# Decoder step on one core: the input projection's first phase in chunks of 256, 384 and 392 tokens, and a three-operand step in the top-k search

## The reference

```
h = rms_norm(x) @ w_in                      # (1032, 1024) x (1024, 4168)
# columns: q 512, k 256, v 256, gate 512, index q 512, index w 8, index k 64, hgrn q/f/i/gate 4x512
score[t, s] = sum over 8 heads of relu(iq[t] . ik[s]) * iw[t]      # s <= t
keep the top 256 of score[t]                 # everything is kept for t < 256
attention over the kept keys, with a relative-position bias
HGRN2 recurrence over q, log-decay, k, v     # 8 heads, 64 x 64 state, chunkwise
y = x + (both branches, gated) @ w_out
```

## Time and profile before

| what | us |
|---|---|
| median of 3 runs | 795.87 |
| the three runs | 795.87, 800.88, 794.12 |
| profiled execution, its own time | 794.41 |
| its span, first to last instruction | 792.4 |
| TensorE busy in the span | 755.5 |
| VectorE / ScalarE / GpSimd busy | 550.4 / 420.8 / 389.2 |

### The profile page before, as it was taken

How to read it: one execution, slowest core, us unless ns; L and a number is a source line. 1 busy time by engine, 2 the same in 40 slices (tenths; PEclk the granted TensorE clock), 3 DMA queues, 4 the chain that set the end, 5 groups by cost and what they waited for, 6 DMA issues and landing times.

```text
span 792.4 us, 20225 instructions
## 1 busy us (share of the span) xinstructions
PE 755.5 (95%) x7576; PEld 699.6 (88%) x7576; DVE 550.4 (69%) x1114; ACT 420.8 (53%) x1274; POOL 389.2 (49%) x572
## 2 busy tenths in 40 slices
PE   3999999999999989999999999989899998999998
PEld 3889989899999989999989999967788877998998
DVE  3644767999989999878997847786746368554121
ACT  6765675336465857768465746654435564421110
POOL 3454735437825296548667255239861427510320
PEclk9999999999999999999999999999999999999999
DMA  8303021211102202041203445395583634441632
GB/s 286 93 21 88 14 88 38 74 55 55 55 2 82 93 23 100 29 128 48 95 2 89 140 115 168 90 284 147 149 242 124 202 124 136 136 131 61 230 95 87
DMA packets 69927, 83.57 MB, mean 105 GB/s; under 512 B 20458, under 2 KB 55962, under 8 KB 69578
## 3 DMA queue, kind: packets, MB, share of 16 engines
q1 hardware_dynamic: 65146, 68.68, 27.7%
q0 software_dynamic: 4688, 13.64, 6.1%
HBM read 64.95 MB, written 17.34 MB: 104 GB/s over the span
## 4 chain that ended last, share of the span: by engine, by line
PE 67%; DVE 11%; issue 8%; ACT 5%; POOL 5%; DMA 3%; SPq 0%; DVEq 0%; ACTq 0%; POOLq 0%
PE psum L2330 16%; PE psum L2327 13%; PE psum L1360 11%; PE psum L2246 4%; PE psum L1293 4%; PE psum L1309 3%; DVE flag_count L2066 2%; POOL w_low L555 2%; DMA page_keys<-in_cache_kt 2%; PE psum L1266 1%; PE psum L1272 1%; PE psum L1270 1%; DVE bit_kept L2079 1%; PE psum L2204 1%; PE psum L2182 1%
## 5 line engine op out<-in xcount | busy, mean ns | idle before, releaser
L2330 PE MATMUL psum<-w_high,xT_high 128*128 128x256 f32 x640 | 183.2, 286 | 3.6 <-ACT psum L1838 3.2
L2330 PE MATMUL psum<-w_low,xT_high 128*128 128x256 f32 x640 | 179.5, 280 | 0.0
L2330 PE MATMUL psum<-w_high,xT_low 128*128 128x256 f32 x640 | 179.3, 280 | 0.0
L555 POOL TENSOR_TENSOR w_low<-w_raw,w_high 128x256 fp32r<-128x256 f32 (+1 forms) x144 | 106.5, 778 | 64.6 <-ACT w_high L1715 55.0
L2330 PEld LDWEIGHTS psum<-w_high,xT_high 128*128 128x128 f32 x640 | 120.3, 188 | 6.2 <-ACT psum L1838 3.8
L2330 PEld LDWEIGHTS psum<-w_high,xT_low 128*128 128x128 f32 x640 | 120.4, 188 | 0.4
L2330 PEld LDWEIGHTS psum<-w_low,xT_high 128*128 128x128 f32 x640 | 120.5, 188 | 0.0
L2327 PE MATMUL psum<-xT_high,w_high 128*128 128x384 f32 (+3 forms) x312 | 102.8, 330 | 1.1 <-POOL w_low L555 1.1
L2327 PE MATMUL psum<-xT_low,w_high 128*128 128x384 f32 (+3 forms) x312 | 99.7, 319 | 0.0
L2327 PE MATMUL psum<-xT_high,w_low 128*128 128x384 f32 (+3 forms) x312 | 99.6, 319 | 0.0
L2066 DVE TENSOR_SCALAR_CACHE_REDUCE flag_count<-scores,candidate 128x512 f16<-128x512 f32 (+2 forms) x96 | 96.8, 1009 | 0.0
(11 more groups left out here) (335 smaller groups left out, 1847.7 us busy)
## 6 DMA issues: line engine op xcount, KB each, us to landing
w_raw<-in_w_main SPq DMA_DIRECT2D x40, 512.0 KB, 5.2
x_rows<-in_x_prompt SPq DMA_DIRECT2D x8, 512.0 KB, 6.0
page_keys<-in_cache_kt SPq DMA_DIRECT2D x32, 128.0 KB, 3.5
page_keys<-in_cache_kt POOLq DMA_DIRECT2D x32, 128.0 KB, 3.4
page_values<-in_cache_v SPq DMA_DIRECT2D x32, 128.0 KB, 3.8
page_values<-in_cache_v POOLq DMA_DIRECT2D x32, 128.0 KB, 3.8
x_res<-in_x_prompt SPq DMA_DIRECT2D x32, 128.0 KB
out<-y_rows SPq DMA_DIRECT2D x32, 128.0 KB
```

The costliest lines, as they stand in the source:

```text
L555: last = gp.tensor_tensor(WL[:, u % 2, 4 * h + k, 0:w], raw(u)[:, h, k, 0:w], f(WH[:, u % 2, 4 * h + k, 0:w]), ALU.subtract)
L2330: last = pe.matmul(ps(BANK[n], w, rows(i)), x[:, k, row0(i):row0(i) + rows(i)], ww[:, sl, k, 0:w], start=first, stop=final)
```

## The change

- Token chunks are 256, 384 and 392 wide instead of 384, 384 and 264.
- The index-query units have no job for the first chunk: seven jobs in the front instead of nine, four T jobs instead of six in the second iq unit. Job numbers after that are lower by four.
- Squares of row tiles 3 and 8 (the samples) are made by VectorE with a multiply-and-reduce of two operands, the other seven stay on ScalarE. ScalarE scales tiles 4 and 7, VectorE the others.
- The transposes of chunk 1 stand in one piece behind job 0, those of chunk 2 in two pieces, inside and behind job 3.
- SyncE starts the page table's two transfers before the weights of unit 1.
- GpSimd's order becomes: split 0, gathers (0; 0, 1), split 1, (0; 2 to 4), constants, split 2, (0; 5 to 7), (1; 0, 1), split 3, (1; 2 to 7), (2; all), (3; all), split 4, diagonal masks. The first job of unit 1 waits for half of split 1 only.
- `sample_index` is behind job 19, the last before unit 4, and its sum behind job 20, the first of unit 4. Three of the samples' flags are summed one job later than the shift by four would put them.
- The kept bit of the search: `tensor_scalar` with a constant and a per-partition scalar becomes `scalar_tensor_tensor` with the bit value broadcast as a second tensor.

```diff
-CHUNKS = [(0, 384), (384, 384), (768, 264)]
+CHUNKS = [(0, 256), (256, 384), (640, 392)]
+CHUNK_ROWS = [(0, 1), (2, 3, 4), (5, 6, 7, 8)]
+SQUARES_BY_ACT = [0, 1, 2, 4, 5, 6, 7]
+ROWS_BY_ACT = [4, 7]
...
-FRONT = [(x, b, c) for c in range(3) for x, b in ((0, 0), (1, 0), (1, 1))]
-IX_JOBS = 7
+FRONT = [(x, b, c) for c in range(3) for x, b in ((0, 0), (1, 0), (1, 1)) if x == 0 or c > 0]
+IX_JOBS = 5
...
-X_AT = {(2, 3): (1, range(4)), (2, 7): (1, range(4, 8)), (4, 7): (2, range(4)), (5, 3): (2, range(4, 8))}
+X_AT = {(0, 7): (1, range(8)), (3, 3): (2, range(4)), (3, 7): (2, range(4, 8))}
...
-        out = [(u, "T", b, c) for c in range(3) for b in range(2)]
+        out = [(u, "T", b, c) for c in (1, 2) for b in range(2)]
...
-GROUPS = {8: [0], 9: [1], 10: [2], 11: [3], 12: [4], 13: [5, 6], 15: [7], 16: [8], 17: [9], 18: [10], 19: [11]}
+GROUPS = {6: [0], 7: [1], 8: [2], 9: [3, 4], 11: [5, 6], 12: [7], 13: [8, 9], 14: [10], 15: [11]}
-KEYS_ROWS_AT, SAMPLE_AT, SAMPLE_SUM_AT = 7, 22, 23
-FLAGS_AT = {29: 0, 36: 1, 42: 2, 46: 3, 49: 4, 53: 5, 72: 6, 77: 7}
+KEYS_ROWS_AT, SAMPLE_AT, SAMPLE_SUM_AT = 5, 19, 20
+FLAGS_AT = {26: 0, 32: 1, 38: 2, 42: 3, 46: 4, 50: 5, 69: 6, 73: 7}
...
             load_x(0)
             sp.dma_start(IDN[:, :], c_ident).then_inc(s["ident_in"], 16)
             load_weights(sp, 0)
...
-            load_weights(sp, 1)
             load_x(1)
-            load_x(2)
...
+            load_weights(sp, 1)
+            load_x(2)
...
             split_w(gp, 0)
-            split_w(gp, 1)
             gp.wait_ge(s["page_rows_in"], 32)
...
-            load_index_keys(0, 0, NPG)
+            load_index_keys(0, 0, 2)
+            gp.wait_ge(s["x_rows_scaled"], 4)
+            split_w(gp, 1)
+            load_index_keys(0, 2, 5)
             gp.wait_ge(s["const_in"], CONSTS_IN)
...
-            load_index_keys(1, 0, 3)
+            split_w(gp, 2)
             gp.wait_ge(s["x_low_ready"], 3 * KC)
             gp.tensor_tensor(XS[:, :, :], f(XH[:, :, T:TT]), f(XL[:, :, T:TT]), ALU.add).then_inc(s["x_sample_ready"], 1)
-            split_w(gp, 2)
-            load_index_keys(1, 3, NPG)
-            load_index_keys(2, 0, 3)
+            load_index_keys(0, 5, NPG)
+            load_index_keys(1, 0, 2)
             split_w(gp, 3)
-            load_index_keys(2, 3, NPG)
+            load_index_keys(1, 2, NPG)
+            load_index_keys(2, 0, NPG)
             load_index_keys(3, 0, NPG)
...
                 if u == 3:
+                    split_w(gp, u + 1)
                     for t in range(2, NT):
...
-                    split_w(gp, u + 1)
...
+            def square(i):
+                r = rows(i)
+                dve.wait_ge(s[f"x_in{i}"], 16)
+                link(dve.tensor_tensor_reduce(CU[0:r, 0:D].bitcast(BF16), x_buf(i)[0:r], x_buf(i)[0:r], 1.0, 0.0, ALU.mult, ALU.add,
+                                              accum_out=STAT[0:r, 0, i:i + 1]))
...
-                    dve.tensor_scalar(HIT[:, 0:6], CNT[:, 0:6], float(TOPK), BITF[:, bass.ds(it, 1)],
-                                      ALU.is_lt, ALU.mult).then_inc(s["dve_chain"], 1)
+                    dve.scalar_tensor_tensor(HIT[:, 0:6], CNT[:, 0:6], float(TOPK), BITF[:, bass.ds(it, 1)].to_broadcast([P, 6]),
+                                             ALU.is_lt, ALU.mult).then_inc(s["dve_chain"], 1)
```

64 lines of the change are left out of this document (32 added, 32 removed).

## The result

The changed kernel took **803.65 us** (median of 15 runs, 795.5 to 808.96), the kernel before 799.13 us (15 runs, 794.12 to 800.88): a ratio of 1.0074, 95% interval [1.0053, 1.0094]. It is slower, by less than 1%, and outside the range of 783 to 801 that was forecast (794.0).

The account below looks back on a forecast made before the run. TensorE, busy 95%, was taken as the bound, with VectorE already setting its time at one place. 794.4 - 11.2 (matmuls) + 0.5 (front) + 5.8 (gathers and split) + 4.5 (VectorE's chain) gave 794.0 us, range 783 to 801.

Parts of the forecast that it names:

- the term of +4.5 us for VectorE's chain: VectorE's search and scans: TensorE waits 4.5 us for them up to pair 1.
- 6.5 us of the kept bit's waits: First 16 search rounds: of 7.9 us of waits above the floor, the new form saves 6.5.
- the front: TensorE up to the second iq unit: that unit starts at 56.2 us, 5.1 of 5.6 us kept, term +0.5.
- GpSimd's row: GpSimd's gathers and splits: split 2 starts at 46.7 us, gathers end at 136.6, then split 4 takes 5.6.
- T: Start of unit 4's first job, which needs split 4: forecast 142.4 us, bounds 136.5 and 152.
- matmuls: TensorE: 4 blocks x 24 matmuls x 256 tokens dropped, 11.2 us less.
- waiting for gathers and split: TensorE idle at `sample_index` and at unit 4's first job: +5.8 us.
- VectorE, the search: VectorE's search starts behind split 4 and the masks, at T + 2.1 = 144.5 us, 7.4 later than before.
- the late T: Rival: GpSimd's stream slower than before; T of 152 gives 803 us; decides from T = 142.8; chance 0.14.
- the bit that waits: Rival: the three-operand kept bit waits as long; 6.5 us come back at the second scan, 800 us; chance 0.12.
- Waits at the pairs: GpSimd's exponents for pair 0 come 11 us late; TensorE loses 4 to 5, its remaining gain at pair 1.
- The work removed stays removed: Rival: gathers end by 130 us, pairs 0 and 1 don't hold TensorE; 783.7 us, or 780.7; chance 0.22.

Follow-up runs that it names:

- after_again: The changed kernel, unedited, run and profiled again: median 807.15 us, ratio 1.0124 to before; its profiled execution took 809.7 us.
- bit_alone: The kernel before with only the kept bit in the new three-operand form: 796.41 us, ratio 0.9970 to before.
- first execution: The first profiled execution of the changed kernel: 795.5 us, the fastest of its 15.
- gaps: The changed kernel with a semaphore link after each GpSimd instruction of decayed keys, index queries' scale and splits: 805.95 us, ratio 1.0098 to before.
- gaps_first: woven_gathers with links between GpSimd's instructions only in the first pair's scale and the split behind it: 784.97 us, ratio 0.9838 to before.
- warm: The changed kernel with matmuls nobody reads, 24 before sample_index's wait and 10 before unit 4's first job: 807.08 us, ratio 1.0104 to before.
- old_bit: The changed kernel with the kept bit back in the old tensor_scalar form: 803.11 us, ratio 1.0058 to before.
- free_gathers: The changed kernel without each gather's wait for the one before it on its buffer: 789.24 us, ratio 0.9898 to before.
- woven_gathers: The changed kernel with the last sixteen gathers taken in turn from the third and fourth buffer, waits kept: 791.22 us, ratio 0.9918 to before.
- gaps_before: The kernel before with links after each GpSimd instruction of decayed keys, index queries' scale and splits: 796.69 us, ratio 0.9994 to before.
- free_before: The kernel before without each gather's wait for the one before it on its buffer: 807.89 us, ratio 1.0141 to before.
- gaps_free: free_gathers with the semaphore links of gaps between GpSimd's instructions: 806.19 us, ratio 1.0109 to before.

## Why the prediction was wrong

The sign of the mechanism was named: GpSimd's gathers late, TensorE idle at `sample_index` and at unit 4's first job. The step that failed is the term of +4.5 us for VectorE's chain. It could be that small only because 6.5 us of the kept bit's waits had been taken off the chain as saved by the new form, and they are not saved: the longest wait is 7.99 us in `after_again` and 7.37 in `bit_alone`, 7.36 before. Two more terms were too small: the front (+0.5 for 3 to 4) and, through it, GpSimd's row, so that T came 5.2 to 6.7 us late. Here is the sum, execution against execution, from the 794.4 us of the profiled one of before; the last term is what the others leave:

| term, us | forecast | first execution | `after_again` |
|---|---|---|---|
| matmuls | -11.2 | -11.2 | -11.2 |
| front | +0.5 | +4.1 | +3.0 |
| waiting for gathers and split | +5.8 | +5.9 | +8.5 |
| VectorE's chain up to pair 1, and all behind | +4.5 | +2.3 | +15.0 |
| sum | -0.4 | +1.1 | +15.3 |

The last term has both causes in it: in `after_again` the second scan stands at 287.94, not at 274.5, of which +6.7 are unit 4 (149.06 for T = 142.4), -0.6 the masks behind it and +7.4 the stretch from search to second scan. In the first execution a bit slipped through, and the term was small. Neither execution is a usual one. Against the median, 803.65, the forecast missed by 9.65 us: 4.7 are the base, since the profiled execution of before lay that far below its median of 799.13 (I had put the difference at 1.5 from three runs), and 4.9 are the mechanism. How these divide between the bit and the late T no run separates: with the bit's waits gone the time fell by 2 us at most in `gaps`, and by some 6 in `gaps_first`, where T was no longer late.

**TensorE's work**: 96 matmuls gone, right. **The start**: 11.10 us, forecast 11.0. **The front**: wrong by 3.6. I had the second iq unit start at 56.2, and it did at 59.83 (58.75 in `after_again`); of the 5.1 us to be kept, 1.5 were (2.6). Chunk 1's transposes began at 22.50, not at 20.5, because ScalarE waited for unit 1's weights, which now come behind the other loads:

```profile
19.02 1.06 ACT L1720 ACTIVATE w_high<-w_raw 128x1024 fp32r<-128x1024 f32 x1 [2.73 <-DMA w_raw<-in_w_main]
```

I had costed the page table's transfers at 1.4 us of SyncE's time and called them covered. SyncE issued unit 1's weights at 8.46 (before at 4.88), behind the page table and behind chunk 1's three tiles of 512 KB, which the prediction does not mention; and just ahead of the wait's end the DMA queues moved 12 GB/s. The kernel before has such a hollow as well, but behind its weights. Windows of the changed kernel and of before, as under `warm`, the last two numbers being the DMA engines' share and GB/s:

```profile
11.50:14.00 2.50, 2.50 (x14) 2.50 (x13) 2.46 (x6) 2.14 (x6) 2.50 (x6) 1.00 0.07 12
```

```profile
17.50:20.00 2.50, 2.50 (x16) 2.03 (x15) 1.86 (x4) 2.50 (x6) 2.50 (x4) 1.00 0.20 40
```

That is argued from the traces; no run had the loads in another order. Another 2 us went in chunk 2 (ix done at 49.7, not 45.6): its two rows of transposes took 2.38 us each where the sum has 1.94, and TensorE waited 0.44 us for the second half of split 1.

**GpSimd**, mis-sized for the same reason. Split 2 began at 50.82, not 46.7: +4.1. The rest of the row was well sized in this execution: five gathers 12.6 us (12.5), split 3 8.16 (7.5), 22 gathers 64.3 us from 77.72 to 142.01 (63.8), split 4 5.5 (the forecast's last addition, 136.6 + 5.6, is 142.2 and not 142.4, which changes nothing). So T = 147.57 in the first execution, and 5.2 us is 4.1 of the front with small change. In `after_again` split 2 began at 49.74 (+3.0), and the row itself took longer: five gathers +0.9, split 3 8.05, 22 gathers 66.06 us (3.00 each, +2.3), so T = 149.06. That a late ScalarE moves GpSimd's whole row, I had not followed further than my own estimate of 46.7.

**VectorE, the search**: T + 1.5 in both executions (2.1). **The kept bit** is the step that failed in kind. "Of these I take 6.5" was a saving that does not exist: 15.0 us for 31 bits in the first execution and 23.3 in the second, before 24.5; 7.99 in one of the second's. Its argument was that line 2082 never took over 0.61 us; but line 2082 runs right behind the bit, when GpSimd's run is over. The row of 7.36 us told the cause, GpSimd's run; what it did not tell is that the form had to do with it, and the rival on this, at 0.12, came true. The Trainium skill, SBUF — State Buffer, "Who interferes with whom", has a VectorE instruction with two SBUF inputs contend with GpSimd's reads: by that rule the new form would still wait, and the runs agree. Where it says that the pair is held for one whole instruction, the wait of 7.99 us, through all that was left of a run of twelve, is longer.

Two rivals came together: the late T (its point was T = 142.8) and the bit that waits. Each was given its own chance, 0.14 and 0.12, and each its own time, 803 and 800, as if one excluded the other; both together give about 807 at the T that was measured. Only with T = 152 would they give 809, so the 809.7 of `after_again` is met by this only roughly. The execution of 795.5 us, which has no long wait at the first pair, is near what the forecast described; it is the fastest of 15, and its like in `old_bit` (795.71) says that this is luck with one bit and not the form.

**Waits at the pairs**: right in place. GpSimd's exponents held ScalarE for 8.10 us at pair 0 (forecast some 10) and 5.71 at pair 1; TensorE lost 2.86 and 0.65 us behind it, less than the 4 to 5 taken. In `after_again` the second of them was 11.06 us and TensorE's wait 4.46.

**"The work removed stays removed"** (783.7): 8.1 us of 11.2 do, in `free_gathers`, against the median of before. Of the missing 3.1, 2.4 are the front's: its second iq unit starts at 58.14, and 61.3 less half of 11.2 is 55.7.

Open: why one kept bit slips into a run of GpSimd (0.41 us at 216.35 in the first execution) and another waits for its end, by what a long row of gathers without waits stalls the other engines, and what another order of SyncE's loads would give back in the front.

## What to carry to other kernels

When an edit shortens the leading engine, follow each other engine's own row to the new meeting point, and start it from the latest work that releases it: here ScalarE's wait of 2.7 us for weights moved a row of 22 gathers that nobody had waited for. Gathers that wait for each other cost 2.9 us apiece, taken in turn over two buffers 1.75 (16 gathers from 94.35 to 122.40 in `woven_gathers`); without any wait between them they went with a stall of other engines in three kernels of four, so two under way, each waiting for the one two back, is what showed a gain and no stall here; three gave more, but one of its four executions took 806.25 us and was not profiled. Where a small instruction waits for another engine's run, put a gap into the run where the chain is critical: gaps everywhere brought 2 us at most, gaps at the first pair about 6. And read more than one execution before a time is explained: the first one profiled here would have confirmed the forecast.

## What the runs showed of the hardware

- A VectorE instruction on 128 x 6 elements waited 7.4 to 8.0 us until a run of GpSimd instructions on SBUF had a gap, in the form with one tensor (7.36 before) and in that with two (7.37 in `bit_alone`, 7.99 in `after_again`); with a semaphore link after each of GpSimd's instructions it took 0.69 us at most in `gaps` and 1.40 in `gaps_before`. Without a link a bit sometimes came through in 0.40 or 0.41 us.
- Beside rows of 11 and 22 indirect gathers issued some 1.25 us apart ScalarE stood for 4.4 us (`free_before`) and 13.5 us (`gaps_free`); in `gaps_free` TensorE's instructions then came in groups of one to five, 0.7 us apart or more. `free_gathers` has such a row without the stall. No kernel whose gathers wait for one another showed it.
- The granted clock, as means of 10 us: 0.58 from 140 to 150 us in `after_again`, where TensorE worked 3.02 us, 0.90 in the next window, 1.00 in the one behind it; 0.60 and 0.55 from 90 to 110 us in `gaps_free`, then 1.00. Matmuls that nobody reads kept it at 1.00 from 140 to 160 us in `warm`, and no saving is shown.
- Executions of one program differ by 13 us (795.5 to 808.96 of the 15). The largest single difference between the two executions that were profiled is one kept bit's wait of 8 us.
